# A value gather by matmul: every second panel as three fp32r passes, 1152 panel columns, five row buffers

## The chip, the cores and the metric

One core of a Trainium2 chip. The time is that of one execution on the device in microseconds (us); lower is better. Of the kernel before there are three timed runs and one profiled execution, which has a time of its own.

## What is computed

One layer of a decoder trunk on 256 + 16 tokens with 2048 features: an input projection, a gated short convolution and a chunkwise mLSTM, an output projection, and then a PEER layer. The change lies in the last part of the PEER layer. For each token, 8 heads choose 16 experts each of 16384, so that there are 128 slots per token; the reference does

```
u = peer_u[eb]
a = jax.nn.gelu(jnp.einsum('td,tkd->tk', xb, u), approximate=False)
return jnp.einsum('tk,tkd->td', wb * a, peer_v[eb])
...
h = layer_norm(ALPHA * h + ffn, ln2_g[l], ln2_b[l])
```

for two blocks ("tiles", T = 0 and 1) of 128 tokens. `peer_v` has 16384 rows (128 keys by 128) of 2048 fp32 values. All data is fp32.

## The kernel before, in words

The last stage computes the sum over slots of coefficient times row of `peer_v`, in two ways at once, by columns.

**Columns 0 to 1103 (FD = 1104), by matmul.** The coefficients are first spread out into a dense matrix of weights, `wt`, 128 x 128 x 128 for each tile: one-hot matrices of the two key indices are made on VectorE and ScalarE (`one_hots`, L1749 and L1309; `key_one_hots`, L1326), multiplied on TensorE (`place`, L935), and copied to `wt0` and `wt1` by ScalarE (`w_copy`, L1336). After that the whole of `peer_v` is streamed in 128 panels of 128 rows. SP loads panel i into `v_raw[i % 5]` (L457 to L468), when panel i - 5 is done; the first five are loaded early. TensorE's `panel(i)` (L971) does 6 fp32 matmuls, 2 tiles by 3 column cuts of 368, with `wt` as the stationary operand, and adds into 6 PSUM banks that `tile_open` (L874) filled with ALPHA * h1. The trace shows each of these fp32 matmuls as two records, 12 for a panel. `panel_done` counts panels.

**Columns 1104 to 2047 (GD = 944), by gather.** GpSimd (POOL) issues one indirect DMA for each of the 256 pairs of tile and slot (`gather_v`, L1938), which brings 128 rows of 944 values into `v_rows[n % 7]` (VRING = 7). VectorE (DVE) does `add_row(n)` (L1765): h1 += coefficient * row, one scalar_tensor_tensor, chained on its own semaphore `v_added`, since each adds to the same accumulator. Gather n waits until add n - 7 is done; gathers 3 and 4 wait for the opening of tiles 0 and 1 (their buffers lie on the part of `h1` that `tile_open` reads), gather 5 for the last one-hot product (its buffer lies on a one-hot buffer).

Each engine does its list in the order written. DVE has nothing but the 256 adds in this stage, ScalarE (ACT) nothing at all, SP the panel loads. Eight panels ahead of the last one SP also loads the two LN2 parameter rows, spread over all partitions, 1024 KB each. After the last add and the last panel DVE does the statistics and the scaling of LN2, and SP writes the output.

Earlier in the same program the projections use the form that the change brings to this stage: ScalarE copies an fp32 block to fp32r (`hi`, in `split_hi`, L992), VectorE subtracts that from the block (`lo`, in `split_lo`, L1376), and TensorE's `group` (L486) does three fp32r matmuls, high by high, high by low and low by high.

Of the kernel before, what the change touches and what calls it, by code (L numbers as in the profile page):

```python
# [16 lines left out]
F32 = mybir.dt.float32  # L17
F32R = mybir.dt.float32r
BF16 = mybir.dt.bfloat16
U32 = mybir.dt.uint32  # L20
ALU = mybir.AluOpType
ACT = mybir.ActivationFunctionType
AX = mybir.AxisListType

P = 128
D = 2048
# [3 lines left out]
NT = SEQ // P  # L30
# [3 lines left out]
PH, NKEY, TOPK = 8, 128, 16  # L34
# [41 lines left out]
BLOCKS = KT // 2  # L76
PER_UNIT = P // 4 // 8

FD = 1104
GD = D - FD  # L80
CW = 368
CUTS = tuple((a, a + CW) for a in range(0, FD, CW))
RAWS = 5
VRING = 7
WB = 4
CHUNKS_T = P // WB
OHR = 3
Y_CUTS = ((FD, D), (0, 2 * CW), (2 * CW, FD))

# [27 lines left out]
def decoder_layer(nc, x, meta_tokens, x_turned, params, w_gates, w_in, b_if, p_a, p_b, w_o, peer_wq, peer_keys, peer_u, peer_v,  # L117
# [5 lines left out]
    with ctx:  # L123
# [12 lines left out]
        def sb(name, shape, dt, at=None):  # L136
            size = int(np.prod(shape[1:])) * mybir.dt.size(dt)
            return nc.alloc_sbuf_tensor_at(name, shape, dt, offset=area(size) if at is None else at)

        KB = 1024  # L140
        a_stream = area(64 * KB)
        a_y = area(16 * KB)
        a_m = area(16 * KB)
        a_x = area(2 * KT * L * 4)
        a_yl = area(16 * KB)
        a_ml = area(16 * KB)
        a_head = area(NB * L * 4 + 10 * KB + 512)
        a_tmp = area(13 * KB)

        a_top = area(8 * KB)  # L150
# [70 lines left out]
        slots_t = sb("slots_t", [P, 3, P], F32, a_head + 12 * KB)  # L221
        neg_key = sb("neg_key", [P, P], F32R, a_head + 12 * KB + 3 * P * 4)

        wt0 = sb("wt0", [P, NKEY, P], F32, a_stream)
        assert a_head == a_ml + 16 * KB == a_yl + 32 * KB == a_x + 34 * KB + 32 * KB
        wt1 = sb("wt1", [P, NKEY, P], F32, a_x + 10 * KB)
        v_homes = [a_y + 8 * KB, a_x, a_x + FD * 4, a_tmp, a_tmp + FD * 4]
        v_raw = [sb(f"v_raw{j}", [P, FD], F32, v_homes[j]) for j in range(RAWS)]
        v_rows = [sb(f"v_rows{j}", [P, GD], F32, at) for j, at in
                  enumerate((a_top, a_top + GD * 4, a_y + 8 * KB + FD * 4, a_m, a_m + D * 4, a_y, a_y + GD * 4))]  # L230
        g2_bc = sb("g2_bc", [P, D], F32, a_stream)
        b2_bc = sb("b2_bc", [P, D], F32, a_stream + 8 * KB)
        y2 = sb("y2", [P, NT, D], F32, a_stream + 16 * KB)
# [52 lines left out]
        ps = ctx.enter_context(nc.psum_tensor("ps", [P, 8, 512], F32))  # L286
# [3 lines left out]
        def S(name):  # L290
            if name not in sems:
                sems[name] = ctx.enter_context(nc.semaphore(name))
            return sems[name]

        for n in ("set_apart ones_ready tok_in0 tok_in1 tok_in2 xt_in0 xt_in1 xt_in2 xt_in3 xt_in4 par_in bif_in gw_in keys_in bc2_in out_done "
                  "raw_in0 raw_in1 raw_in2 raw_in3 hi_ready lo_ready halves_used block_done "
                  "blocks_evacuated const_ready ln0_stats ln0_rstd mean_ready rstd_ready ln0_means ln0_rstds ln0_scaled gw_hi gw_lo x32_ready "
                  "x_split gate_w_used gates_read gate_mid gate_log gate_rows "
                  "gate_bc gate_bc_read run_ready run_out run_in pool_chain dve_chain act_chain args_ready "
                  "weights_ready masked v_transposed scores_done v_copied probs_ready num_done "  # L300
                  "recip_ready ssq_ready rms_ready hm_done hm_transposed hmt_written cc_ready sig_ready "
                  "m32_ready hi_part y_ready merged_ready tile0_done gate_used merged_used sum_ready sum_transposed merged_hi "
                  "merged_lo res_done res_ready wo_added ln1_stats ln1_rstd "
                  "ln1_nmr xn1_ready xn1_transposed h32_ready h1_turned h1_ready wq_tile wq_used wq_block "
                  "q_copied q_turned qs_ready qk_done sc_copied topk_neg topk_exp topk_done u_in0 u_in1 u_in2 u_in3 "
                  "u_in4 u_in5 u_in6 u_in7 v_in0 v_in1 v_in2 v_in3 v_in4 v_in5 v_in6 dots_done gelu_ready coef_ready "
                  "scaled tile_opened ut_turned ut_copied ut_used acc_scaled slots_turned slots_copied diff_ready "
                  "one_hot_squares one_hot_units oh_ready oh_dve_ready w_done w_evac vr_in0 vr_in1 vr_in2 vr_in3 vr_in4 "
                  "panel_done v_added ln2_stats ln2_rstd ln2_half y2_ready").split():
            S(n)  # L310
        def set_apart(eng):
# [8 lines left out]
        vr_in = [S(f"vr_in{j}") for j in range(RAWS)]  # L320
# [42 lines left out]
        def key_number(c):  # L363
            return (c - CHUNKS_T) // 2 if c >= CHUNKS_T and c % 2 else None

        def wt_rows(T, i, n):

            return (wt1 if T else wt0)[:, i:i + n, :]

        FIRST_HEADS = ((0, (0, 1)), (0, (2, 3)), (1, range(NB)))  # L370

# [110 lines left out]
        def _(pe):  # L482
# [488 lines left out]
            def panel(i):  # L971

                pe.wait_ge(vr_in[i % RAWS], 16 * (i // RAWS + 1))
                for T in range(NT):
                    for n, (a, b) in enumerate(CUTS):
                        last = mm(ps[:, 3 * T + n, 0:CW], wt_rows(T, i, 1)[:, 0, :], v_raw[i % RAWS][:, a:b], False,
                                  i == NKEY - 1)
                last.then_inc(S("panel_done"), 1)
# [7 lines left out]
        def _(act):  # L986
            chain = Steps(act, S("act_chain"))

            def A(o, i, f, **kw):
                return nc.scalar.activation(o, i, f, **kw)  # L990
# [335 lines left out]
            def key_one_hots(c):  # L1326

                act.wait_ge(S("w_done"), c - OHR + 1)
                o = oh[c % OHR]
                act.wait_ge(S("diff_ready"), key_number(c) + 1)  # L1330
                A(o[:, 1, :, :], ps[:, 5, :].rearrange("p (q i) -> p q i", q=WB), ACT.Square
                  ).then_inc(S("one_hot_squares"), 1)
                act.wait_ge(S("one_hot_squares"), CHUNKS_T + key_number(c) + 1)
                A(o[:, 1, :, :], o[:, 1, :, :], ACT.Relu, scale=-1.0, bias=one[:, 0:1]).then_inc(S("oh_ready"), 1)

            def w_copy(c):  # L1336

                act.wait_ge(S("w_done"), c + 1)
                t0 = c % CHUNKS_T * WB
                src = ps[:, 6 + (c + 1) % 2, :].rearrange("p (q i) -> p i q", q=WB)  # L1340
                A((wt0 if c < CHUNKS_T else wt1)[:, :, t0:t0 + WB], src, ACT.Copy).then_inc(S("w_evac"), 1)

            for u in range(1, 2 * PH):
                if u > FIRST_PAIR_UNIT:
# [20 lines left out]
            for c in range(CHUNKS_T, 2 * CHUNKS_T):  # L1365
                w_copy(c)
                if c % 2 == 0 and c + OHR < 2 * CHUNKS_T:
                    key_one_hots(c + OHR)


        @block.vector
        def _(dve):
            chain = Steps(dve, S("dve_chain"))
            V = nc.vector
# [374 lines left out]
            def one_hots(c):  # L1749

                dve.wait_ge(S("w_done"), c - OHR + 1)
                o = oh[c % OHR]
                t0 = c % CHUNKS_T * WB
                if key_number(c) is None:
                    V.tensor_tensor(o[:, 1, :, :], iota[:, :].unsqueeze(1).to_broadcast([P, WB, P]),  # L1755
                                    slots_t[:, 2, t0:t0 + WB].unsqueeze(2).to_broadcast([P, WB, P]), ALU.is_equal)
                for q in range(WB):
                    ins = V.tensor_scalar(o[:, 0, q, :], iota[:, :], slots_t[:, 1, t0 + q:t0 + q + 1],  # L1758
                                          slots_t[:, 0, t0 + q:t0 + q + 1], ALU.is_equal, ALU.mult)
                ins.then_inc(S("oh_dve_ready"), 1)  # L1760
# [4 lines left out]
            def add_row(n):  # L1765

                T, s = divmod(n, SLOTS)
                dve.wait_ge(v_in[n % VRING], 16 * (n // VRING + 1))
                if s:
                    dve.wait_ge(S("v_added"), n)  # L1770
                else:
                    dve.wait_ge(S("acc_scaled"), T + 1)
                V.scalar_tensor_tensor(h1[:, T, FD:D], v_rows[n % VRING][:, :], coef_all[:, T, s:s + 1], h1[:, T, FD:D],  # L1773
                                       ALU.mult, ALU.add).then_inc(S("v_added"), 1)
# [38 lines left out]
            dve.wait_ge(S("slots_copied"), 2)  # L1813
            for c in range(CHUNKS_T, 2 * CHUNKS_T):
                one_hots(c)
            for n in range(NT * SLOTS):
                add_row(n)


# [34 lines left out]
        def _(pool):  # L1854
# [83 lines left out]
            def gather_v(n):  # L1938

                if n >= VRING:  # L1940
                    pool.wait_ge(S("v_added"), n - VRING + 1)
                elif n in (3, 4):
                    pool.wait_ge(S("tile_opened"), n - 2)
                elif n == 5:
                    pool.wait_ge(S("w_done"), 2 * CHUNKS_T)
                set_apart(pool)
                Q.indirect_dma_start(v_rows[n % VRING][:, :], None, v_gathered,  # L1947
                                     bass.IndirectOffsetOnAxis(ap=idx_all[:, n:n + 1], axis=0)
                                     ).then_inc(v_in[n % VRING], 16)
# [62 lines left out]
```

## Time and profile before

| what | value |
|---|---|
| median of 3 runs | 2341.24 us (2339.43 to 2343.64) |
| the profiled execution's own time | 2348.28 us |
| its span, first to last instruction | 2346.4 us |
| PE (TensorE matmul) busy in the span | 1973.0 us, 84% |
| DVE busy | 1562.4 us, 67% |
| POOL busy | 949.0 us, 40% |
| ACT busy | 833.1 us, 36% |
| moved by DMA | 678.45 MB |

The page cuts the span into 40 slices of 58.7 us and gives the busy tenths of each; PEclk is the clock granted to TensorE, in tenths of its full speed. The stage of the change is the last nine slices or so: TensorE works there at full clock without a break, all DMA engines are busy, ScalarE is idle. "busy" of an engine counts instructions in execution; for TensorE these overlap, so its pace is read from the starts. "issue" in front of an instruction is time in which the engine waited for nothing that the profile shows. A KB in the DMA rows is 1024 bytes, a GB/s is 10^9 bytes per second.

### The profile page before, as it was taken

How to read it: one execution, taken by the hardware profiler on the slowest of the kernel's cores; microseconds unless marked ns; L12 is line 12 of the kernel's file. 1: busy time of each engine (PE TensorE's matmuls, PEld its weight loads, DVE VectorE, ACT ScalarE, POOL GpSimd, SP SyncE). 2: the span in 40 equal slices, each digit the busy share in tenths (PEclk: the TensorE clock that was granted, in tenths of full speed). 3: DMA queues.
4: the chain of work that ended last, by engine and by line, in shares of the span. 5: the costliest groups of instructions: out<-in, count | busy, mean ns of one | idle time of the engine just before them, and what ended most of it. 6: DMA issues, size and time to landing. Idle time of an engine off the chain costs nothing.

```text
span 2346.4 us, 30017 instructions
## 1 busy us (share of the span) xinstructions
PE 1973.0 (84%) x10559; PEld 1617.7 (69%) x10559; DVE 1562.4 (67%) x2234; ACT 833.1 (36%) x1369; POOL 949.0 (40%) x560
## 2 busy tenths in 40 slices
PE   8999999999999999999974242456446999999995
PEld 8888899998889988888763231345445766666663
DVE  7444455555445554554899999999988766666667
ACT  6444443444444444445122121586767300000000
POOL 0000000000000000000558888888874488788874
PEclk9999999999999999999997566676667999999998
DMA  7544465565565565556999999999996499999996
GB/s 245 162 143 142 141 197 184 177 181 186 191 196 180 180 197 182 195 179 233 380 390 377 421 412 412 406 421 416 418 421 261 190 412 411 411 409 411 411 410 274
DMA packets 213884, 678.45 MB, mean 289 GB/s; under 512 B 14712, under 2 KB 64256, under 8 KB 180224
## 3 DMA queue, kind: packets, MB, share of 16 engines
q0 software_dynamic: 57664, 394.31, 41.4%
q1 hardware_dynamic: 156112, 282.75, 35.8%
q8 instruction: 62, 1.02, 0.2%
q14 instruction: 46, 0.38, 0.0%
HBM read 674.89 MB, written 2.11 MB: 289 GB/s over the span
## 4 chain that ended last, share of the span: by engine, by line
PE 46%; issue 23%; POOL 11%; DMA 11%; DVE 8%; ACT 1%; DVEq 0%; POOLq 0%; ACTq 0%
PE ps L484 45%; DMA u_rows<-in_peer_u,idx_all 8%; POOL v_rows L1947 7%; POOL u_rows L1934 4%; DMA v_rows<-in_v_gathered,idx_all 2%; DVE junk L1725 2%; DVE ohs L1758 1%; DVE h L1773 1%; ACT hi L990 0%; DVE ohs L1755 0%; DVE ki L1678 0%; DVE scw L1679 0%; DVE ki L1685 0%; ACT h1t L990 0%; PE ps L625 0%
## 5 line engine op out<-in xcount | busy, mean ns | idle before, releaser
L1380 DVE TENSOR_TENSOR lo<-raw,hi 128x1024 fp32r<-128x1024 f32 x344 | 419.5, 1225 | 478.6 <-ACT hi L990 478.0
L1934 POOL DMA_INDIRECT u_rows<-in_peer_u,idx_all x256 | 532.6, 2081 | 153.2 <-issue 67.1
L990 ACT ACTIVATE hi<-raw 128x1024 fp32r<-128x1024 f32 x348 | 368.2, 1060 | 533.4 <-PE ps L484 532.1
L1725 DVE SCALAR_TENSOR_TENSOR junk<-u_rows,h 128x2048 bf16<-128x2048 f32 x228 | 520.0, 2282 | 45.1 <-DMA u_rows<-in_peer_u,idx_all 44.8
L484 PE MATMUL ps<-v_raw,wt 128*128 128x368 f32 x1536 | 477.1, 474 | 2.0 <-DMA v_raw<-in_peer_v 1.9
L1947 POOL DMA_INDIRECT v_rows<-in_v_gathered,idx_all x256 | 394.1, 1539 | 145.3 <-issue 79.5
L484 PE MATMUL ps<-xh,hi 128*128 128x256 f32 (+2 forms) x1536 | 438.9, 286 | 1.2 <-issue 0.9
L484 PE MATMUL ps<-xh,lo 128*128 128x256 f32 (+2 forms) x1536 | 435.2, 283 | 0.0
L484 PE MATMUL ps<-xl,hi 128*128 128x256 f32 (+2 forms) x1536 | 434.4, 283 | 0.0
L1773 DVE SCALAR_TENSOR_TENSOR h<-v_rows,coef_all,h 128x944 f32<-128x944 f32 x256 | 307.6, 1202 | 176.8 <-DMA v_rows<-in_v_gathered,idx_all 174.9
L484 PEld LDWEIGHTS ps<-v_raw,wt 128*128 128x128 f32 x1536 | 292.4, 190 | 186.7 <-DMA v_raw<-in_peer_v 2.5
L1874 POOL TENSOR_TENSOR rstd<-rstd,m_half 128x1 f32<-128x1 f32 (+1 forms) x7 | 5.4, 764 | 818.6 <-DVE rstd L1643 798.5
L484 PEld LDWEIGHTS ps<-xh,hi 128*128 128x128 f32 x1536 | 289.9, 189 | 6.5 <-issue 5.6
L484 PEld LDWEIGHTS ps<-xl,hi 128*128 128x128 f32 x1536 | 290.2, 189 | 0.0
L484 PEld LDWEIGHTS ps<-xh,lo 128*128 128x128 f32 x1536 | 289.6, 189 | 0.0
L903 PE MATMUL ps<-ident,u_rows 128*128 128x128 f32 x448 | 81.2, 321 | 182.9 <-issue 158.8
L484 PE MATMUL ps<-ohs 128*128 128x128 f32 x512 | 101.2, 361 | 128.2 <-ACT ohs L990 126.2
L903 PEld LDWEIGHTS ps<-ident,u_rows 128*128 128x128 f32 x448 | 68.3, 170 | 197.4 <-issue 188.7
L484 PEld LDWEIGHTS ps<-ohs 128*128 128x128 f32 x512 | 88.9, 259 | 142.6 <-ACT ohs L990 136.5
L990 ACT ACTIVATE ut<-ps 128x512 f32<-128x512 f32 x112 | 66.9, 597 | 263.8 <-PE ps L903 261.7
L484 PE MATMUL ps<-ut,h1t 128*128 128x256 f32 x448 | 131.4, 426 | 0.1
L484 PE MATMUL ps<-hi,xh 128*128 128x512 f32 x256 | 101.7, 397 | 1.8 <-DVE t_y L1558 1.3
(224 smaller groups left out, 2364.3 us busy)
## 6 DMA issues: line engine op xcount, KB each, us to landing
raw<-in_w_in SPq DMA_DIRECT2D x96, 1024.0 KB, 5.3
v_raw<-in_peer_v SPq DMA_DIRECT2D x128, 552.0 KB, 7.7
raw<-in_w_in SPq DMA_DIRECT2D x64, 256.0 KB, 3.3
raw<-in_w_in SPq DMA_DIRECT2D x32, 512.0 KB, 4.7
raw<-in_p_a SPq DMA_DIRECT2D x16, 1024.0 KB, 5.0
raw<-in_p_b SPq DMA_DIRECT2D x16, 1024.0 KB, 5.1
raw<-in_w_o SPq DMA_DIRECT2D x16, 1024.0 KB, 5.1
wq_raw<-in_peer_wq SPq DMA_DIRECT2D x16, 1024.0 KB, 9.7
```

Source lines behind the costliest of these rows:

```text
L484: return nc.tensor.matmul(o, a, b, start=start, stop=stop)
L903: last = nc.tensor.transpose(ps[:, 3 + g % 2, (2 * n + r) * P:(2 * n + r + 1) * P], u_rows[row_slot(u, k)][:, kt * P:(kt + 1) * P], ident[ ...
L990: return nc.scalar.activation(o, i, f, **kw)
L1380: V.tensor_tensor(raw_lo[:, hh // 2, k4, :] if kept else lo[:, hh % SLOT_N, :, :], raw[:, hh // 2, k4, :], (kept_hi(hh) if kept else hi[:, ...
L1725: V.scalar_tensor_tensor(junk[:, n % 2, :], u_rows[row_slot(u, k)][:, :], 1.0, h1[:, u // PH, :], ALU.mult, ALU.mult, accum_out=dots[:, u ...
L1758: ins = V.tensor_scalar(o[:, 0, q, :], iota[:, :], slots_t[:, 1, t0 + q:t0 + q + 1], slots_t[:, 0, t0 + q:t0 + q + 1], ALU.is_equal, ALU.mult)
L1773: V.scalar_tensor_tensor(h1[:, T, FD:D], v_rows[n % VRING][:, :], coef_all[:, T, s:s + 1], h1[:, T, FD:D], ALU.mult, ALU.add).then_inc(S(" ...
L1874: Q.tensor_tensor(rstd[:cnt, n:n + 1], rstd[:cnt, n:n + 1], m_half[:cnt, 0:1], ALU.pow).then_inc(S(name + "_rstd"), 1)
L1934: Q.indirect_dma_start(u_rows[slot][:, :], None, peer_u, bass.IndirectOffsetOnAxis(ap=idx_all[:, n:n + 1], axis=0)).then_inc(u_in[slot], 16)
L1947: Q.indirect_dma_start(v_rows[n % VRING][:, :], None, v_gathered, bass.IndirectOffsetOnAxis(ap=idx_all[:, n:n + 1], axis=0)).then_inc(v_in ...
```

## The change

- FD goes from 1104 to 1152 columns: matmul cuts of 384, panels of 576 KB, gathered rows of 896 columns. VRING goes from 7 to 5; the two row buffers that lay on `h1` are dropped, for the high parts of v (`v_hi`, two buffers) lie there now. `wt0` and `wt1` become two ends of one tensor, so that one instruction can read panel i's weights of both tiles.
- For each odd panel i (64 of them, numbered n = i // 2), ACT copies `v_raw` (1152 columns) to `v_hi` in fp32r and the weights of both tiles (2 x 128) to `w_hi`; it waits for the panel's load and for panel i - 4, which used the same `v_hi`. DVE subtracts the high parts, v in place over `v_raw` (`v_lo`), the weights into `w_lo`. TensorE does 18 fp32r matmuls of 384 columns (2 tiles, 3 passes, 3 cuts) in place of 6 fp32 matmuls. Even panels stay fp32.
- DVE's two subtractions for panel i stand amid the adds: panel 1 ahead of add 2, panel 3 ahead of add 4, then panel 5 ahead of add 6, panel 7 ahead of add 10, and so on each fourth add, up to panel 127 ahead of add 250. So panel i is split ahead of add 2i - 4.
- Gather 3 now waits for the last one-hot product, so three gathers go out early; then gather n waits for add n - 5.

The diff (semaphore names, `wt_rows` and `w_copy`'s renamed target left out):

```diff
-FD = 1104
+FD = 1152
-CW = 368
+CW = 384
-VRING = 7
+VRING = 5
...
+        v_lo = [sb(f"v_lo{j}", [P, FD], F32R, v_homes[j]) for j in range(RAWS)]
         v_rows = [sb(f"v_rows{j}", [P, GD], F32, at) for j, at in
-                  enumerate((a_top, a_top + GD * 4, a_y + 8 * KB + FD * 4, a_m, a_m + D * 4, a_y, a_y + GD * 4))]
+                  enumerate((a_top, a_top + GD * 4, a_y + 8 * KB + FD * 4, a_y, a_y + GD * 4))]
+        v_hi = [sb(f"v_hi{j}", [P, FD], F32R, a_m + j * D * 4) for j in range(2)]
+        w_hi = [sb(f"w_hi{j}", [P, NT, P], F32R, a_head + (8 + j) * KB) for j in range(2)]
+        w_lo = [sb(f"w_lo{j}", [P, NT, P], F32R, a_head + (10 + j) * KB) for j in range(2)]
...
+        def split_number(i):
+            return i // 2 if i % 2 else None
...
                 pe.wait_ge(vr_in[i % RAWS], 16 * (i // RAWS + 1))
+                if split_number(i) is not None:
+                    b = split_number(i) % 2
+                    pe.wait_ge(S("v_lo_ready"), split_number(i) + 1)
+                    for T in range(NT):
+                        for w, v in ((w_hi[b], v_hi[b]), (w_hi[b], v_lo[i % RAWS]), (w_lo[b], v_hi[b])):
+                            for n, (c0, c1) in enumerate(CUTS):
+                                last = mm(ps[:, 3 * T + n, 0:CW], w[:, T, :], v[:, c0:c1], False,
+                                          i == NKEY - 1 and w is w_lo[b])
+                    last.then_inc(S("panel_done"), 1)
+                    return
...
+            def split_panel(i):
+
+                n = split_number(i)
+                if n < 2:
+                    act.wait_ge(S("tile_opened"), n + 1)
+                else:
+                    act.wait_ge(S("panel_done"), i - 4 + 1)
+                act.wait_ge(vr_in[i % RAWS], 16 * (i // RAWS + 1))
+                A(v_hi[n % 2][:, :], v_raw[i % RAWS][:, :], ACT.Copy)
+                if n == 0:
+                    act.wait_ge(S("w_done"), 2 * CHUNKS_T)
+                    act.wait_ge(S("w_evac"), 2 * CHUNKS_T)
+                A(w_hi[n % 2][:, :, :], wt_tiles(i), ACT.Copy).then_inc(S("v_hi_ready"), 1)
...
+            def split_panel(i):
+
+                n = split_number(i)
+                dve.wait_ge(S("v_hi_ready"), n + 1)
+                V.tensor_tensor(v_lo[i % RAWS][:, :], v_raw[i % RAWS][:, :], v_hi[n % 2][:, :].bitcast(F32), ALU.subtract)
+                V.tensor_tensor(w_lo[n % 2][:, :, :], wt_tiles(i), w_hi[n % 2][:, :, :].bitcast(F32), ALU.subtract
+                                ).then_inc(S("v_lo_ready"), 1)
+
             for n in range(NT * SLOTS):
+                if n == 2:
+                    split_panel(1)
+                elif n == 4:
+                    split_panel(3)
+                elif 4 < n < 2 * NKEY - 4 and n % 4 == 2:
+                    split_panel((n + 2) // 2 + 1)
                 add_row(n)
...
                 if n >= VRING:
                     pool.wait_ge(S("v_added"), n - VRING + 1)
-                elif n in (3, 4):
-                    pool.wait_ge(S("tile_opened"), n - 2)
-                elif n == 5:
+                elif n == 3:
                     pool.wait_ge(S("w_done"), 2 * CHUNKS_T)
```

## Rows read from the trace of the kernel before

**Rows 1.** The page: slices of the span (58.7 us each).
```profile
PE   8999999999999999999974242456446999999995
DVE  7444455555445554554899999999988766666667
PEclk9999999999999999999997566676667999999998
GB/s 245 162 143 142 141 197 184 177 181 186 191 196 180 180 197 182 195 179 233 380 390 377 421 412 412 406 421 416 418 421 261 190 412 411 411 409 411 411 410 274
```

**Rows 2.** Windows: us; busy PE, PEld, DVE, ACT, POOL (records); clock, DMA share, GB/s.
```profile
400.00:500.00 100.00, 100.00 (x836) 99.66 (x835) 52.98 (x61) 41.04 (x43) 0.00 (x0) 1.00 0.60 183
600.00:700.00 100.00, 100.00 (x437) 81.84 (x436) 46.70 (x41) 45.54 (x45) 0.00 (x0) 1.00 0.58 189
1291.00:1350.00 59.00, 15.31 (x72) 12.87 (x72) 55.85 (x103) 8.50 (x14) 47.68 (x25) 0.59 1.01 421
1900.00:2280.00 380.00, 380.00 (x1231) 233.53 (x1230) 241.96 (x202) 0.00 (x0) 311.36 (x203) 1.00 1.02 410
```

**Rows 3.** Waits, 1900 to 2280 us: who for whom, us, times, longest.
```profile
DVE h L1773 <- DMA v_rows<-in_v_gathered,idx_all: 137.9, 201, 1.8
```

**Rows 4.** DMA issues of the page: KB each, median us to landing.
```profile
v_raw<-in_peer_v SPq DMA_DIRECT2D x128, 552.0 KB, 7.7
```

**Rows 5.** Groups from 1842 us on: busy us, mean ns of one, idle before.
```profile
L484 PE MATMUL ps<-v_raw,wt 128*128 128x368 f32 x1536 | 477.1, 474 | 2.0 <-DMA v_raw<-in_peer_v 1.9
L1845 DVE SCALAR_TENSOR_TENSOR y<-h,mv,g_bc 128x944 f32<-128x944 f32 x2 | 2.4, 1200 | 0.0
L1845 DVE SCALAR_TENSOR_TENSOR y<-ps,mv,g_bc 128x736 f32<-128x736 f32 x2 | 2.0, 980 | 0.0
```

**Rows 6.** Groups, 400 to 500 us.
```profile
L484 PE MATMUL ps<-xh,hi 128*128 128x258 f32 x191 | 54.2, 284 | 0.0
L1380 DVE TENSOR_TENSOR lo<-raw,hi 128x1024 fp32r<-128x1024 f32 x35 | 42.5, 1225 | 44.1 <-ACT hi L990 44.0
L990 ACT ACTIVATE hi<-raw 128x1024 fp32r<-128x1024 f32 x35 | 37.1, 1060 | 54.0 <-PE ps L484 53.9
```

**Rows 7.** Timeline of TensorE, the first and the last of 13 matmuls in a row.
```profile
600.42 0.40 PE L484 MATMUL ps<-hi,xh 128*128 128x512 f32 x1
...
603.20 0.40 PE L484 MATMUL ps<-hi,xh 128*128 128x512 f32 x1
```

**Rows 8.** Group of VectorE, 1300 to 1600 us.
```profile
L1708 DVE TENSOR_TENSOR ohv<-oh_k,kif 128x256 f32<-128x256 f32 x15 | 5.7, 415 | 0.0
```

**Rows 9.** Timeline of the steady stage: start us, us, engine, what, idle before.
```profile
2053.47 1.20 DVE L1773 SCALAR_TENSOR_TENSOR h<-v_rows,coef_all,h 128x944 f32<-128x944 f32 x1 [0.50 <-DMA v_rows<-in_v_gathered,idx_all]
2054.09 1.40 POOL L1947 DMA_INDIRECT v_rows<-in_v_gathered,idx_all  x1 [0.30 <-issue]
2055.45 1.20 DVE L1773 SCALAR_TENSOR_TENSOR h<-v_rows,coef_all,h 128x944 f32<-128x944 f32 x1 [0.78 <-DMA v_rows<-in_v_gathered,idx_all]
2055.79 1.68 POOL L1947 DMA_INDIRECT v_rows<-in_v_gathered,idx_all  x1 [0.30 <-issue]
```

**Rows 10.** Timeline of the stage's start.
```profile
1842.52 5.17 DVE L1773 SCALAR_TENSOR_TENSOR h<-v_rows,coef_all,h 128x944 f32<-128x944 f32 x4
...
1844.57 40.77 PE L484 MATMUL ps<-v_raw,wt 128*128 128x368 f32 x131
1845.31 1.89 POOL L1947 DMA_INDIRECT v_rows<-in_v_gathered,idx_all  x1 [43.19 <-PE ps L484]
...
1850.43 1.20 DVE L1773 SCALAR_TENSOR_TENSOR h<-v_rows,coef_all,h 128x944 f32<-128x944 f32 x1 [2.74 <-DMA v_rows<-in_v_gathered,idx_all]
```

**Rows 11.** Timeline of the stage's end.
```profile
2295.67 27.93 PE L484 MATMUL ps<-v_raw,wt 128*128 128x368 f32 x84 [1.93 <-DMA v_raw<-in_peer_v]
...
2316.62 10.34 DVE L1773 SCALAR_TENSOR_TENSOR h<-v_rows,coef_all,h 128x944 f32<-128x944 f32 x8 [0.87 <-DMA v_rows<-in_v_gathered,idx_all]
...
2327.00 1.45 DVE L1832 BATCH_NORM_STATS2 st<-ps 128x6 f32<-128x368 f32 x3
```

More of the change, by code:

```diff
@@ L222, in decoder_layer @@
         neg_key = sb("neg_key", [P, P], F32R, a_head + 12 * KB + 3 * P * 4)
-        wt0 = sb("wt0", [P, NKEY, P], F32, a_stream)
         assert a_head == a_ml + 16 * KB == a_yl + 32 * KB == a_x + 34 * KB + 32 * KB
-        wt1 = sb("wt1", [P, NKEY, P], F32, a_x + 10 * KB)
         v_homes = [a_y + 8 * KB, a_x, a_x + FD * 4, a_tmp, a_tmp + FD * 4]
         v_raw = [sb(f"v_raw{j}", [P, FD], F32, v_homes[j]) for j in range(RAWS)]
+        v_lo = [sb(f"v_lo{j}", [P, FD], F32R, v_homes[j]) for j in range(RAWS)]
         v_rows = [sb(f"v_rows{j}", [P, GD], F32, at) for j, at in
-                  enumerate((a_top, a_top + GD * 4, a_y + 8 * KB + FD * 4, a_m, a_m + D * 4, a_y, a_y + GD * 4))]
+                  enumerate((a_top, a_top + GD * 4, a_y + 8 * KB + FD * 4, a_y, a_y + GD * 4))]
+        v_hi = [sb(f"v_hi{j}", [P, FD], F32R, a_m + j * D * 4) for j in range(2)]
+        w_hi = [sb(f"w_hi{j}", [P, NT, P], F32R, a_head + (8 + j) * KB) for j in range(2)]
+        w_lo = [sb(f"w_lo{j}", [P, NT, P], F32R, a_head + (10 + j) * KB) for j in range(2)]
+        wt_gap = (a_x + 10 * KB - a_stream) // (P * 4)
+        wt_both = sb("wt_both", [P, wt_gap + NKEY, P], F32, a_stream)
         g2_bc = sb("g2_bc", [P, D], F32, a_stream)
@@ L305, in decoder_layer @@
                   "q_copied q_turned qs_ready qk_done sc_copied topk_neg topk_exp topk_done u_in0 u_in1 u_in2 u_in3 "
-                  "u_in4 u_in5 u_in6 u_in7 v_in0 v_in1 v_in2 v_in3 v_in4 v_in5 v_in6 dots_done gelu_ready coef_ready "
+                  "u_in4 u_in5 u_in6 u_in7 v_in0 v_in1 v_in2 v_in3 v_in4 dots_done gelu_ready coef_ready "
                   "scaled tile_opened ut_turned ut_copied ut_used acc_scaled slots_turned slots_copied diff_ready "
-                  "one_hot_squares one_hot_units oh_ready oh_dve_ready w_done w_evac vr_in0 vr_in1 vr_in2 vr_in3 vr_in4 "
+                  "one_hot_squares one_hot_units oh_ready oh_dve_ready w_done w_evac vr_in0 vr_in1 vr_in2 vr_in3 vr_in4 v_hi_ready v_lo_ready "
                   "panel_done v_added ln2_stats ln2_rstd ln2_half y2_ready").split():
@@ L364, in key_number, with wt_tiles @@
             return (c - CHUNKS_T) // 2 if c >= CHUNKS_T and c % 2 else None
+        def split_number(i):
+            return i // 2 if i % 2 else None
+        def wt_tiles(i):
+            return wt_both[:, i:i + wt_gap + 1:wt_gap, :]
         def wt_rows(T, i, n):
-            return (wt1 if T else wt0)[:, i:i + n, :]
+            return wt_both[:, T * wt_gap + i:T * wt_gap + i + n, :]
         FIRST_HEADS = ((0, (0, 1)), (0, (2, 3)), (1, range(NB)))
@@ L1340, in w_copy @@
                 src = ps[:, 6 + (c + 1) % 2, :].rearrange("p (q i) -> p i q", q=WB)
-                A((wt0 if c < CHUNKS_T else wt1)[:, :, t0:t0 + WB], src, ACT.Copy).then_inc(S("w_evac"), 1)
+                A(wt_rows(c // CHUNKS_T, 0, NKEY)[:, :, t0:t0 + WB], src, ACT.Copy).then_inc(S("w_evac"), 1)
             for u in range(1, 2 * PH):
@@ L1368, in _ @@
                     key_one_hots(c + OHR)
+            def split_panel(i):
[10 more added lines that the diff above has]
+                A(w_hi[n % 2][:, :, :], wt_tiles(i), ACT.Copy).then_inc(S("v_hi_ready"), 1)
+            for i in range(NKEY):
+                if split_number(i) is not None:
+                    split_panel(i)
         @block.vector
```

## The prediction

> **What bounds the kernel now.** I read the page's slices first [rows 1]: before the last nine slices nothing changes, so only the stage from about 1842 us on counts. There TensorE is full, VectorE two thirds busy, and the DMA engines move about 410 GB/s. The windows come next [rows 2]: in the 380 us from 1900 to 2280, 1231 matmul records and 202 adds, DMA share 1.02. So a panel takes 12 x 380 / 1231 = 3.70 us on TensorE, and two adds (a panel's worth: 256 adds to 128 panels) take 2 x 380 / 202 = 3.76 us. The third view is the waits [rows 3]: 201 of the 202 adds wait for their gather, 137.9 us in all. TensorE hardly waits for its panels (1.9 us in the stage, [rows 5]), which land 7.7 us after issue [rows 4] with 5 buffers of 3.7 us each. So two bounds lie on one another: TensorE at 7.41 us for two panels, and DMA, through the gathers, at 7.52 us. The last add ends at 2326.96, the last matmul at about 2323.6 [rows 11], and LN2 starts at 2327.00. The adds, and so DMA, set the end, TensorE 3.4 us behind. A change has to relieve both.
>
> **The change, part by part,** in units of two panels and four adds (64 units).
>
> *TensorE.* An fp32 matmul of 368 columns starts every 2 x 308.7 ns; at 384 columns a record takes 308.7 x 384 / 368 = 322 ns, a full panel 12 x 0.322 = 3.86 us. For the split panel: fp32r matmuls of 256 to 258 columns start every 100 / 836 = 119.6 ns, those of 512 columns, by the starts of the 1st and the 13th of a run, every (603.20 - 600.42) / 12 = 232 ns [rows 2, 6, 7]. Between them, 384 columns take 175 ns, and 18 of them 3.15 us. A unit is 7.01 us against 7.41. TensorE gains 0.40 x 64 = 26 us, if nothing holds it. Alone it is worth nothing, since DMA ends last.
>
> *DMA.* A unit moves 2 x 552 + 4 x 472 = 2992 KB now (944 columns x 4 bytes x 128 rows are 472 KB), and 2 x 576 + 4 x 448 = 2944 KB after: a factor of 0.984. From add 4 at 1850.43 to add 248 at 2316.62 [rows 10, 11] it is 466.2 us; 1.6% of it is **7.5 us less**. At 7.40 us for a unit DMA stays the bound; TensorE has 0.39 us to spare.
>
> *Early loads.* Now 4 rows and 5 panels are in before the stage (4 adds run at once, the fifth waits, [rows 10]): 4648 KB. After: 3 rows and 5 panels, 4224 KB. The 424 KB move into the stage: 434 kB / 410 GB/s = **1.1 us more**.
>
> *VectorE.* Adds: 944 against 736 columns cost 1200 and 980 ns [rows 5], 1.06 ns a column, so 896 columns take 1.15 us. Eight adds back to back took 10.34 us, so 1.305 from start to start [rows 11]: 1.25 after. Subtraction: 1024 columns at 1225 ns [rows 6], 1152 at 1.36 us; 256 columns at 0.42 [rows 8], of which some 0.35 shows behind another. A split is 1.7 us. A unit: 4 x 1.25 + 1.7 = 6.7 us of 7.40. VectorE goes from 70% (5.22 of 7.52) to 91%, still under the bound; the cover is its 0.7 us of waiting in each unit. The last eight adds are 0.05 shorter each: **0.4 less**. Without the DMA bound it would be TensorE at 7.01 that is next, then VectorE at 6.7.
>
> *ScalarE* has nothing to do in the stage. 1152 columns at 1060 ns per 1024 [rows 6] are about 1.2 us, 256 more about 0.4: 1.6 us of 7.4. It matters as latency. The raw panel i is ordered when panel i - 5 ends, lands up to 7.7 us later, is copied (1.6) and subtracted (1.7): 11.0 us, plus semaphores. TensorE wants it 4 panels, 14.8 us, after the order. About 3.5 us to spare, and VectorE may come to the split anywhere in that interval; where it comes early it waits, and the adds behind it, and the gathers behind these.
>
> *POOL and the ring.* Here a price is unknown. In the steady stage a gather ends 0.82 us after the end of the add that ran when it started (2054.67 to 2055.49, 2056.65 to 2057.47, [rows 9]), and the next starts 0.30 later. So the slot of an add that ends at t is refilled by a gather that ends near t + 2.7 (1.12 to its start, a mean of 311.36 / 203 = 1.53 in it, [rows 2]). The longest hold grows from an add of 1.20 to a subtraction of 1.36. The round trip of a row is 7 x 1.88 = 13.2 us now, of which 1.2 add, 2.7 POOL, 9.3 landing and queue. After it has to be 5 x 1.85 = 9.25 us: 1.15 add, 2.7 POOL, **5.4 us for the landing**. The nearest quick one is at the start: gather 4 ends at 1847.20, its add starts at 1850.43, 3.2 us [rows 10]. What lies between 3.2 and 9.3 is queue: now about 5 rows and 2 panels are in flight, 3.5 MB, which is 8.5 us at 410 GB/s. With two rows fewer and a panel sooner on its way, some 1.9 MB (2.4 rows, 1.4 panels) are left, 4.6 us, and DMA stays fed. I take 1 us for all losses of coupling and for the start, where the splits of panels 1 and 3 fall between adds while the ring fills. Ends: 0 (the rings smooth it all) and 20 us (the second rival).
>
> The shared port of VectorE and GpSimd gives those holds a name: by the Trainium skill (SBUF — State Buffer, "SBUF: two separate sides") a VectorE operation with two SBUF inputs locks out a GpSimd operation that reads SBUF until it ends. The rows agree with it on the adds; by it each of the 128 subtractions is one more hold, and the sum would lose what the ring cannot take up, as in the second rival.
>
> *Before the stage:* 4% more columns in the 12 matmuls that open the tiles, of 5.8 us for ten at the lower clock, gives **0.2 more**. Output, LN2: the same columns in other cuts, nothing.
>
> **Sum:** -7.5 + 1.1 - 0.4 + 1.0 + 0.2 = -5.6 us. Against the profiled execution's own 2348.28 us (span 2346.4 and 1.9 around it) that is 2342.7; it was 7.0 us above the median of the runs, so against 2341.24 it is **2335.6 us**, 0.24% faster. I count 0.2% (4.7 us) as what a measurement can tell from no change.
>
> **Rivals.**
>
> *A higher rate of DMA.* Rows of 2048 columns in the u stage moved at 421 GB/s, at a DMA share of 1.01 [rows 2]; the 1104 and 944 columns move at 410. If 1152 and 896 columns run like those, a unit is 7.40 x 410 / 421 = 7.21 us, still above TensorE's 7.01: 64 x 0.19 = 12 us more, 2323.5. For it: 1152 and 896 columns are whole multiples of 256 bytes, 1104 and 944 are not. Against: the u rows are also longer, 8 KB apiece, and their stage runs on other work. 0.15. The Trainium skill has such a rule (DMA: Bandwidth & Descriptors, "How a descriptor splits into AXI transactions": a descriptor that starts off a 256-byte boundary fetches unused bytes); the trace shows only the two rates and not their cause.
>
> *The ring of five starves (slower).* Place: a gather's landing in the steady stage. It decides from 5.4 us on. At 5.8 us a row needs (1.15 + 2.7 + 5.8) / 5 = 1.93 us instead of 1.85, and 252 rows 20 us more: 2355.6. For it: 9.3 us of landing today, and a pause of 1.7 us at each split, behind which rows queue up and then want new gathers at once. TensorE, held by splits that stand among late adds, follows. Against: the queue shrinks with what is in flight. 0.28.
>
> *The gain is lost without a loss.* VectorE at 91% must take each gather when it lands; its waits on a late high part plus the ring eat 3 to 8 us, and the time stays within 2337 to 2344. 0.12.
>
> *That the change does not do what it says* (fp32r passes as dear as fp32 ones) would show as 18 x 0.64 us for a panel; the projections' pace excludes it. Nor should TensorE's clock fall: the slices show it low only where TensorE was 20 to 60% busy, and 0.9 where it was 70% busy [rows 1]; here it will be 95% busy, with short gaps.
>
> **How the numbers follow.** Forecast case 0.45: 2331 to 2340, two thirds of it faster by over 0.2%, one third within (0.30 and 0.15). Higher rate 0.15, all faster. Starved ring 0.28, slower. Lost gain 0.12: 0.05 faster, 0.07 within. Sum: faster 0.50, within 0.2% 0.22, slower 0.28. The range goes from the second case's 2323.5 to most of the third: 2323 to 2354. The likeliest case's own is 2331 to 2340.
>
> **What would show it.** In the profile after: DMA share still 1.02 at 410 GB/s, 4 adds in 7.4 us, adds that wait on gathers for about 0.7 us a unit in all, matmul starts at 0.322 and 0.175 us, short waits of TensorE of 0.4 us a unit, full clock. Wrong: a DMA share of 0.97 or less with VectorE waiting on gathers (starved ring), VectorE waiting on ScalarE ahead of its subtractions (late high parts), a rate near 421 (second case), TensorE without waits (my prices for it too low).

## The result, and the profile after

The changed kernel takes 2362.24 us (median of 6 runs, 2359.16 to 2366.42) against 2342.93 us for the kernel before (6 runs): ratio 1.0087, 95% interval 1.0076 to 1.0098. It is 19.3 us **slower**. The forecast was 5.6 us faster, and the range ended at 2354. The case that came about is the rival with the ring of five, at a price near the one given for it (20 us).

The slices of the page after, to be laid beside [rows 1]:

```profile
PE   8999999999999999999964424455557999999985
DVE  7444455554444545554899999999989787778777
PEclk9999999999999999999987666667577999999998
GB/s 243 165 138 142 145 198 176 194 162 201 189 195 180 190 183 196 182 187 248 394 369 409 422 416 419 415 414 416 399 421 155 296 391 394 378 391 395 379 384 263
```

Up to slice 30 nothing of weight has changed. In the last nine slices the granted clock is still full, VectorE is busier, as meant, and the rate of DMA has dropped from 410 to somewhere between 378 and 395 GB/s. The windows from 1850 to 1900 and 1900 to 2280 us give it exactly (columns as in [rows 2]):

```profile
1850.00:1900.00 50.00, 48.17 (x207) 36.74 (x206) 36.21 (x36) 10.32 (x14) 28.32 (x25) 1.00 1.00 387
1900.00:2280.00 380.00, 354.07 (x1470) 262.74 (x1469) 299.16 (x294) 72.15 (x98) 247.22 (x196) 1.00 1.00 387
```

Against [rows 2] this is the whole result in one line. VectorE's 294 operations are 98 of the splits and 196 adds, where there were 202 in the same time: four adds take 4 x 380 / 196 = 7.76 us instead of 7.52. Note the DMA share: 1.00 after, 1.02 before. It counts the time that packets take, and looks full in both; only the GB/s tell that 6% of the rate is gone. TensorE is busy 354 us of 380 and waits for the rest.

Who waits for whom, 1900 to 2280 us (us in total, times, longest), beside [rows 3]:

```profile
ACT v_hi L1010 <- DMA v_raw<-in_peer_v: 291.4, 46, 10.5
POOL v_rows L1997 <- DVE h L1811: 92.3, 67, 2.6
DVE h L1811 <- DMA v_rows<-in_v_gathered,idx_all: 76.8, 105, 2.1
...
POOL v_rows L1997 <- issue: 40.8, 129, 1.8
PE ps L494 <- DVE w_lo L1859: 25.7, 33, 2.5
...
```

ScalarE's wait costs nothing; it has nothing else to do. The second and the third row belong together. Before, POOL waited 3.4 us for VectorE in this window, that is, a free buffer was nearly always there. Now it waits 92.3 us for an add to free one, and VectorE waits 76.8 us for a row to land. That fits a ring of row buffers that is too short, each end waiting for the other and the DMA engines between them with too little to do. By themselves these two rows do not show it, though: the version with seven buffers below, which keeps DMA full, has 76.9 and 62.9 us in them. What sets the changed kernel apart is the rate of 387 GB/s. TensorE comes third, it waits for splits that stand among the late adds.

The landings after (from issue, median us), and the chain that ended last, 1900 to 2340 us, with four of its longest pieces:

```profile
v_raw<-in_peer_v SPq DMA_DIRECT2D x128, 576.0 KB, 7.5
v_rows<-in_v_gathered,idx_all POOLq DMA_INDIRECT x256, 7.4
```

```profile
by line: DMA v_rows<-in_v_gathered,idx_all 49.2%; issue 22.8%; DVE h L1811 15.1%; POOL v_rows L1997 6.6%; DMA v_raw<-in_peer_v 3.1%; DVE w_lo L1859 2.4%; PE ps L494 2.0%; DVE v_lo L1858 0.3%; ACT v_hi L1010 0.3%; POOLq L318 0.1%; ACT w_hi L
...
2048.22 8.70 DMA v_rows<-in_v_gathered,idx_all
2056.94 1.16 DVE h L1811
2058.29 1.90 POOL v_rows L1997
2063.14 8.02 DMA v_rows<-in_v_gathered,idx_all
```

Landing, add, POOL, landing: the chain runs through the round trip of a row buffer. (Between the third and the fourth line POOL issues the gathers that piled up behind its wait, at 2058.29, 2060.49, 2061.89 and 2063.14.) A row takes 380 / 196 = 1.94 us, so five buffers go round in 9.69 us: about 7.4 from issue to landing, 1.15 in the add, 1.1 from the add's end to the next issue (median). The forecast needed 9.25.

One turn of it in the timeline of the steady stage after:

```profile
2056.94 1.15 DVE L1811 SCALAR_TENSOR_TENSOR h<-v_rows,coef_all,h 128x896 f32<-128x896 f32 x1 [2.12 <-DMA v_rows<-in_v_gathered,idx_all]
2058.01 1.35 DVE L1858 TENSOR_TENSOR v_lo<-v_raw,v_hi 128x1152 fp32r<-128x1152 f32 x1
2058.29 1.90 POOL L1997 DMA_INDIRECT v_rows<-in_v_gathered,idx_all  x1 [2.64 <-DVE h L1811]
2059.19 1.16 ACT L1010 ACTIVATE v_hi<-v_raw 128x1152 fp32r<-128x1152 f32 x1 [7.64 <-DMA v_raw<-in_peer_v]
2059.28 0.42 DVE L1859 TENSOR_TENSOR w_lo<-wt_both,w_hi 128x256 fp32r<-128x256 f32 x1
2059.62 2.40 DVE L1811 SCALAR_TENSOR_TENSOR h<-v_rows,coef_all,h 128x896 f32<-128x896 f32 x2
2059.84 1.30 PE L494 MATMUL ps<-v_hi,w_hi 128*128 128x384 f32 x3 [2.48 <-DVE w_lo L1859]
```

VectorE waits 2.12 us for a row, adds it, and turns to the split, while the next two rows land and have to wait for it (the two adds at 2059.62 run back to back). POOL waited 2.64 us for a free buffer; the gather that it then issues at 2058.29 is held by the subtraction that runs from 2058.01 to 2059.36, and ends 0.82 us behind it, at 2060.19. TensorE waits 2.48 us for the same split. Short windows around that wait:

```profile
2059.00:2063.00 4.00, 3.16 (x10) 3.19 (x11) 3.19 (x5) 1.47 (x2) 3.22 (x3) 0.59 0.89 310
2064.00:2068.00 4.00, 4.00 (x16) 2.67 (x15) 2.93 (x4) 1.47 (x2) 2.62 (x3) 1.00 0.93 353
```

DMA moves 310 and 353 GB/s here, and the granted clock behind the wait is 0.59, mostly at the lower of its two levels (1.2 GHz), before it is full again. In the 380 us the clock rounds to 1.00, so this is rare.

### The profile page after: what moved, and what is told of

It reads as the page before. It is cut to its first block, busy times and chain, and to the rows that moved or that the text cites. A ratio compares the mean times of both kernels' runs of the same rounds, so it can differ in the third digit from the quotient of the medians.

```text
span 2363.2 us, 31170 instructions
## 1 busy us (share of the span) xinstructions
PE 1954.7 (83%) x10943; PEld 1666.7 (71%) x10943; DVE 1647.3 (70%) x2362; ACT 926.7 (39%) x1497; POOL 886.6 (38%) x560
## 4 chain that ended last, share of the span: by engine, by line
PE 46%; DMA 19%; issue 17%; DVE 11%; POOL 5%; ACT 1%; SPq 0%; DVEq 0%; POOLq 0%; ACTq 0%
PE ps L494 45%; DMA v_rows<-in_v_gathered,idx_all 10%; DMA u_rows<-in_peer_u,idx_all 8%; POOL u_rows L1986 4%; DVE h L1811 3%; DVE junk L1763 2%; POOL v_rows L1997 1%; DVE ohs L1796 1%; DMA v_raw<-in_peer_v 1%; DVE w_lo L1859 0%; ACT hi L1010 0%; DMA raw<-in_w_in 0%; DVE ohs L1793 0%; DVE ki L1716 0%; DVE scw L1717 0%
## 5 line engine op out<-in xcount | busy, mean ns | idle before, releaser
L1986 POOL DMA_INDIRECT u_rows<-in_peer_u,idx_all x256 | 540.2, 2110 | 145.4 <-issue 68.7
L1763 DVE SCALAR_TENSOR_TENSOR junk<-u_rows,h 128x2048 bf16<-128x2048 f32 x228 | 519.6, 2280 | 44.2 <-DMA u_rows<-in_peer_u,idx_all 42.8
L1997 POOL DMA_INDIRECT v_rows<-in_v_gathered,idx_all x256 | 324.2, 1266 | 236.0 <-DVE h L1811 129.8
L1811 DVE SCALAR_TENSOR_TENSOR h<-v_rows,coef_all,h 128x896 f32<-128x896 f32 x256 | 294.6, 1151 | 109.6 <-DMA v_rows<-in_v_gathered,idx_all 102.9
L494 PE MATMUL ps<-v_raw,wt_both 128*128 128x384 f32 x768 | 258.3, 486 | 0.0
L1010 ACT ACTIVATE v_hi<-v_raw 128x1152 fp32r<-128x1152 f32 x64 | 74.6, 1166 | 396.8 <-DMA v_raw<-in_peer_v 367.1
L494 PEld LDWEIGHTS ps<-v_raw,wt_both 128*128 128x128 f32 x768 | 144.8, 190 | 85.5 <-ACT wt_both L1010 0.7
```

What stands on the lines that cost most here:

```text
L494: return nc.tensor.matmul(o, a, b, start=start, stop=stop)
L1763: V.scalar_tensor_tensor(junk[:, n % 2, :], u_rows[row_slot(u, k)][:, :], 1.0, h1[:, u // PH, :], ALU.mult, ALU.mult, accum_out=dots[:, u ...
L1986: Q.indirect_dma_start(u_rows[slot][:, :], None, peer_u, bass.IndirectOffsetOnAxis(ap=idx_all[:, n:n + 1], axis=0)).then_inc(u_in[slot], 16)
```

## The experiments

Two theories at first. **R**: five row buffers starve the gathers by themselves. **S**: VectorE's pause at each split does it. All ratios are to the kernel before, run beside on the same chip.

### Five buffers in the kernel before

```diff
-VRING = 7
+VRING = 5
...
-                  enumerate((a_top, a_top + GD * 4, a_y + 8 * KB + FD * 4, a_m, a_m + D * 4, a_y, a_y + GD * 4))]
+                  enumerate((a_top, a_top + GD * 4, a_y + 8 * KB + FD * 4, a_y, a_y + GD * 4))]
...
-                elif n in (3, 4):
-                    pool.wait_ge(S("tile_opened"), n - 2)
-                elif n == 5:
+                elif n == 3:
```

> The kernel before with five row buffers instead of seven (gather 3 waits for the last one-hot product, gather n for add n - 5), nothing else. Theory R (the ring of five alone starves the gathers): a row's round trip cannot shrink below about 9.5 us, so a row takes 1.9 us or a little more and the time is 2352 to 2362 us, the DMA rate of the steady stage falls below 400 GB/s. Rival S (VectorE's pause at each split does it, the ring alone is harmless): 2343 to 2347 us, rate 408 to 411.

Measured: 2358.69 us, ratio 1.0070 (1.0053 to 1.0086), 16 us slower. No split, no new column, and most of the loss is there. (One row fewer is loaded early too, 483 kB, an estimated 1.2 us at 410 GB/s.) The window and the landings of this run, and TensorE's last piece and the last add:

```profile
1900.00:2280.00 380.00, 380.00 (x1230) 233.52 (x1229) 232.93 (x195) 0.00 (x0) 272.10 (x195) 1.00 1.01 401
...
v_rows<-in_v_gathered,idx_all POOLq DMA_INDIRECT x256, 7.4
...
2299.79 17.79 PE L484 MATMUL ps<-v_raw,wt 128*128 128x368 f32 x57
2337.22 1.20 DVE L1773 SCALAR_TENSOR_TENSOR h<-v_rows,coef_all,h 128x944 f32<-128x944 f32 x1 [0.24 <-DMA v_rows<-in_v_gathered,idx_all]
```

195 adds, 5 x 380 / 195 = 9.74 us for the trip, the same 7.4 us of landing. TensorE keeps its pace here, since no panel waits for a place among the adds. So the panels run ahead: the last matmul ends at 2317.6, the last add at 2338.4, and from 2320 to 2340 us the rows alone move 236 GB/s. That is why the window still shows 401 GB/s, where a rate below 400 was expected: with 97.5 panels, as many as go with 195 adds, in place of 102.5 it would be an estimated 393. R holds; S alone is out.

### Seven buffers in the changed kernel

```diff
-VRING = 5
+VRING = 7
...
-        v_homes = [a_y + 8 * KB, a_x, a_x + FD * 4, a_tmp, a_tmp + FD * 4]
+        v_homes = [a_y + 8 * KB, a_x, a_x + FD * 4, a_top, a_y]
+        a_late = a_head + 12 * KB
...
+                  enumerate((a_y + 8 * KB + FD * 4, a_top + FD * 4, a_late + GD * 4, a_late + 2 * GD * 4,
+                             a_late + 3 * GD * 4, a_late, a_y + FD * 4))]
...
-                elif i == 3:
-                    sp.wait_ge(S("dots_done"), 2 * PH * TOPK)
+                elif i == 4:
+                    sp.wait_ge(S("w_done"), 2 * CHUNKS_T)
...
-                elif n == 3:
+                elif n == 2:
+                    pool.wait_ge(S("dots_done"), 2 * PH * TOPK)
+                elif n == 5:
                     pool.wait_ge(S("w_done"), 2 * CHUNKS_T)
```

> The changed kernel with seven row buffers: same columns, same splits, the buffers laid out anew (two panels and five rows ahead of the last one-hot product; panel 4 now waits for that product too). Theory R: the round trip may last 13 us again, DMA is full, 2328 to 2340 us. Rival S: VectorE's pauses stay, 2352 to 2362 us.

Measured: 2340.04 us, ratio 0.9991 (0.9982 to 1.0001). 22.2 us come back. (By its trace four panels, where the text above says two, and five rows are ordered ahead of the last one-hot product, 4544 KB; that is 320 KB more than in the changed kernel, an estimated 0.8 us.) Its window, waits and landing:

```profile
1900.00:2280.00 380.00, 368.18 (x1535) 273.02 (x1533) 311.20 (x305) 75.12 (x102) 255.77 (x204) 1.00 1.02 407
...
POOL v_rows L2002 <- DVE h L1814: 76.9, 51, 4.0
DVE h L1814 <- DMA v_rows<-in_v_gathered,idx_all: 62.9, 99, 1.8
...
v_raw<-in_peer_v SPq DMA_DIRECT2D x128, 576.0 KB, 8.2
v_rows<-in_v_gathered,idx_all POOLq DMA_INDIRECT x256, 10.4
```

DMA is at 407 GB/s and a share of 1.02, four adds take 7.45 us, and a landing may last 10.4 us without harm. The time lies at the upper end of what was expected.

### No subtraction, with five and with seven buffers

```diff
-                    pe.wait_ge(S("v_lo_ready"), split_number(i) + 1)
+                    pe.wait_ge(S("v_hi_ready"), split_number(i) + 1)
...
-                if n == 2:
-                    split_panel(1)
...
```

> The changed kernel with VectorE's two subtractions left out; TensorE does its 18 fp32r matmuls on the high parts alone, so the low parts are missing from the result. Five row buffers. Theory R: little is won, 2352 to 2362 us. Rival S: without the pauses 2328 to 2340 us.

> The seven-buffer version (1152 columns) with VectorE's two subtractions left out; TensorE does its 18 matmuls on the high parts, so the low parts are missing from the result. With five buffers leaving them out gave 5 us back. Theory R: with seven buffers DMA is the bound and the pauses are hidden, 2336 to 2341 us (the seven-buffer version: 2340.0). Rival S2 (the pauses cost on their own): 2333 us or less.

Measured with five: 2356.78 us, 1.0057 (1.0040 to 1.0074), 5.5 us less than the changed kernel. With seven: 2338.73 us, 0.9979 (0.9970 to 0.9989), 1.3 us less than the seven-buffer version, which these runs hardly tell. With seven buffers the pauses are all but hidden, though VectorE is 82% busy by the window of that version (311.20 of 380). The window with five buffers and no subtraction:

```profile
1900.00:2280.00 380.00, 375.67 (x1605) 291.07 (x1604) 217.81 (x190) 78.59 (x107) 265.61 (x188) 0.99 1.01 399
```

The 5.5 us are not simply the price of the pauses. Without the subtractions there are 190 adds in the window, fewer than the 196 with them; what goes faster is TensorE, with 1605 records where there were 1470, for the edit also unties a panel from its place among the adds. TensorE then ends at 2294.4, the last add at 2337.2, and in that tail the rows alone move 304 GB/s at most (2310 to 2320 us). So the rate of 399 GB/s against 387 is panels taken sooner, not rows. The ring of five costs 16 us in the kernel before, 18 without the subtractions (2356.78 less 2338.73) and 22 with them: most of the loss is the ring's own. How much of the rest is the pauses and how much the tie, no run here tells.

### Six buffers, in both kernels

In the changed kernel a sixth home on the one-hot scratch, with three rows and five panels early as before; in the kernel before one home fewer.

```diff
-VRING = 5
+VRING = 6
...
-        v_homes = [a_y + 8 * KB, a_x, a_x + FD * 4, a_tmp, a_tmp + FD * 4]
+        a_late = a_head + 12 * KB
+        v_homes = [a_y + 8 * KB, a_x, a_x + FD * 4, a_late + GD * 4, a_late + (GD + FD) * 4]
...
-                  enumerate((a_top, a_top + GD * 4, a_y + 8 * KB + FD * 4, a_y, a_y + GD * 4))]
+                  enumerate((a_top, a_top + GD * 4, a_y + 8 * KB + FD * 4, a_y, a_y + GD * 4, a_late))]
```

> The changed kernel with six row buffers (the sixth on a part of the one-hot scratch, panels 3 and 4 moved up behind it), three rows early as before. Theory R (threshold): a row's round trip of about 9.7 us at five buffers leaves room once 6 x 1.86 = 11.2 us are allowed, so most of the loss comes back: 2339 to 2346 us, landing from issue 8.5 to 9 us. Rival P (each buffer brings its share, half of the 22 us): 2350 to 2354 us.

> The kernel before with six row buffers instead of seven. Five gave 16 us more. Theory R (threshold between five and six): 2341 to 2346 us. Rival P (a share for each buffer): 2349 to 2352 us.

Measured: 2341.07 us, 0.9993 (0.9984 to 1.0003), and 2341.01 us, 0.9989 (0.9980 to 0.9998). All of the loss comes back with one buffer, and the seventh adds nothing that these runs can tell. Landing from issue in the changed kernel: 7.4 us with five, 8.6 with six, 10.4 with seven. With six:

```profile
1900.00:2280.00 380.00, 368.09 (x1528) 271.40 (x1528) 311.44 (x306) 73.67 (x100) 257.18 (x204) 1.00 1.02 405
...
v_rows<-in_v_gathered,idx_all POOLq DMA_INDIRECT x256, 8.6
```

Rival P, a share for each buffer, is out: it is a threshold, between five and six. Since the early loads are those of the changed kernel here, the step from six buffers to five costs 2362.2 - 2341.1 = 21 us in it.

### The other two parts, each alone, with seven buffers

Splits alone (FD = 1104, CW = 368), then columns alone (FD = 1152, `split_number` always None, no `split_panel` on VectorE):

> The splits alone: the seven-buffer layout at the old 1104 panel columns, every second panel in three fp32r passes. TensorE is relieved (6.7 us of 7.5 in a unit), DMA moves the same 2992 KB a unit. Theory D (DMA was the bound before, TensorE only lay beside it): 2341 to 2347 us, no gain. Rival T (TensorE was the true bound): 2330 us or less.

> The columns alone: seven buffers, 1152 panel columns, every panel in fp32, no split. TensorE needs 7.7 us a unit, 64 units: 494 us, where the whole stage took 482. Theory: TensorE binds, 2353 to 2360 us, DMA share about 0.99. Rival (TensorE's pace was set by DMA even so): 2341 us or less.

Measured: 2343.27 us, 1.0005 (0.9996 to 1.0015), and 2357.75 us, 1.0069 (1.0052 to 1.0086). Their windows, in this order:

```profile
1900.00:2280.00 380.00, 353.46 (x1523) 264.84 (x1522) 317.44 (x303) 73.10 (x102) 257.52 (x203) 1.00 1.02 411
...
1900.00:2280.00 380.00, 380.00 (x1180) 223.89 (x1179) 242.96 (x212) 0.00 (x0) 310.75 (x211) 1.00 1.02 407
...
2336.32 1.49 DVE L1881 BATCH_NORM_STATS2 st<-ps 128x6 f32<-128x384 f32 x3 [34.95 <-PE ps L497]
```

In the first, TensorE is idle 26 us of 380 and nothing is faster: DMA was a bound of its own. In the second, 1180 records in 380 us are 0.322 us each, 3.86 for a panel; TensorE binds and is 15 us late. In the same window 212 adds were done, so the gathers ran ahead, and at the end VectorE waits 34.95 us for TensorE's last panel. The DMA share was 1.02 even so, not the 0.99 expected: while the gathers run ahead, DMA is full as well. Both halves of the change are needed together, as the forecast had it.

### More columns

> As the seven-buffer version, with 1176 panel columns: a unit of two panels and four rows is 2920 KB instead of 2944, TensorE 7.16 us instead of 7.01, rows of 3488 and 4704 bytes, no multiples of 256. If bytes alone count: 3 to 4 us faster than the seven-buffer version with 1152 columns. If rows on 256-byte boundaries are faster (rate above 411 GB/s with 1152): slower than that version by 5 us or more.

> Seven buffers, splits, 1200 panel columns: 2896 KB a unit, TensorE 18 x 0.182 + 12 x 0.336 = 7.31 us against DMA's 7.3. If bytes alone count, as the step from 1152 to 1176 suggests (2.4 us per 24 columns): 2335 us. If TensorE now binds: 2338 to 2342 us.

Measured: 1176 columns 2337.62 us, 0.9976 (0.9967 to 0.9986); 1200 columns 2338.33 us, 0.9985 (0.9976 to 0.9995). From 1152 to 1176 it is 2.4 us where 3 to 4 were expected; from 1176 to 1200 nothing that these runs can tell. The rate is 407 GB/s with 1152, 1176 and 1200 alike, so 256-byte boundaries bring nothing that can be seen. With 1104 columns it was 411 in the same layout, and the columns alone, without splits, had 407: the rate falls with the step from 1104 to 1152 columns, and no run here shows why. At 1200 TensorE has no idle time left:

```profile
1900.00:2280.00 380.00, 380.00 (x1562) 288.87 (x1561) 314.07 (x312) 77.16 (x102) 252.49 (x209) 1.00 1.02 407
```

### A version that beats both

```diff
-                if i == NKEY - 8:
+                if i == NKEY - 1:
```

on top of seven buffers, splits and 1176 columns; and the same edit alone in the kernel before.

> Meant to beat both kernels: seven buffers, splits, 1176 panel columns, and the two LN2 parameter rows (2 MB) loaded behind the last panel instead of behind panel 120. There DMA has time to spare. If DMA is the bound until the last panel is loaded: 2 MB at 407 GB/s are 5.2 us, and 2332 to 2334 us against 2337.6. If the end hangs on the last adds alone: 2336 to 2338 us.

> The kernel before with the LN2 parameter rows loaded behind the last panel, nothing else, to tell that edit's share. If the 5 us of DMA count here as well: 2336 to 2339 us. If TensorE's own 479 us of panels hold the end: 2340 to 2343 us.

Measured: 2335.43 us, 0.9960 (0.9947 to 0.9974), 7.9 us under the 2343.31 of the kernel before beside it and 27 under the changed one; and 2341.95 us, 0.9991 (0.9982 to 1.0000). The late load brings some 2 us of the 5 that were possible, hardly more than these runs can tell; in the kernel before its gain is within that. The estimate of 2332 to 2334 was too good. By the trace, DMA does not yet have time to spare behind the last panel's order: the parameter rows are asked for at 2291.2 us, the last gather starts at 2303.3, and a gather of 2295.99 lands 12.12 us later. That the parameter rows delay these last gathers is a reading of the trace, which no run here tests.

## Why the prediction was wrong, point by point

- **Two bounds on one another, TensorE and DMA.** Right. Splits alone gave nothing, columns alone cost 15 us.
- **TensorE's price.** Right. A unit of a full and a split panel was put at 7.01 us; the timeline after has 6.99 (a full panel starts at 1848.33 and the next at 1855.32, with no wait between):

```profile
1848.33 4.03 PE L494 MATMUL ps<-v_raw,wt_both 128*128 128x384 f32 x12
...
1855.32 4.03 PE L494 MATMUL ps<-v_raw,wt_both 128*128 128x384 f32 x12
```

- **VectorE's price.** Right: adds of 1.151 us, subtractions of 1.352 and 0.418, where 1.15, 1.36 and 0.42 stood.
- **DMA's gain of 7.5 us, less 1.1 for the early loads.** Right in sign, too large. With the ring out of the way and the early loads equal in number, the step from 1104 to 1152 columns is 2343.3 to 2340.0, 3.2 us, where 7.5 stood. The forecast kept the rate; it fell from 411 to 407 GB/s, 1% of 466 us or some 4.6 us, and four adds take 7.45 us, not 7.40. That two more steps of 24 columns gave -2.4 and +0.7 us shows where TensorE takes over.
- **The step that failed: "I take 1 us for all losses of coupling", in the part on POOL and the ring.** It measured 21 us (five buffers against six), a little beyond the upper end of 20. The condition was put rightly: a row's landing must come down to 5.4 us behind POOL's end, or the ring starves. What was wrong is the value. I took the 9.3 us of before for a queue that would shrink to 4.6 us with what is in flight, for rows and panels alike. It shrank to 7.4 from issue, some 6.1 behind POOL's mean of 1.27: 0.7 us more than allowed, and the panels' landing hardly shrank, 7.7 us before, 7.5 after. So 7.5 / 3.88 = 1.9 panels and 6.1 / 1.94 = 3.1 rows are on their way, where the forecast had left 1.4 and 2.4. In the forecast's own terms, 5.4 needed, 6.1 found; POOL's part was 2.4 (1.1 and 1.27) and not 2.7, so the trip is 9.69 and not 9.25, and 252 rows at 0.09 us more make about 22 us. The rival priced 5.8 at 20 us, about the price that came.
- **The weighing.** The ends of that cost lay 20 us apart, and the value was put beside the lower one, on an argument about queues that no row supported. The one row for a quick landing (3.2 us, [rows 10]) came from a moment when at first no panel was on its way: five were in, and the sixth is ordered at 1848.6. The row of the same stage said 9.3, and halfway would already have been over the threshold. That the rival came out near its price is in part luck: it put 5.8 us of landing and 2.7 of POOL where 6.1 and 2.4 were found. The range, too, should have reached to what that rival priced, 2355.6, and beyond; it stopped at 2354.
- **The sign named for a starved ring,** a DMA share of 0.97 or less, did not come: the share was 1.00. What told was the rate.
- **The higher rate of DMA.** Out: 407 GB/s at 1152, 1176 and 1200 columns, less than the 411 at 1104. By the Trainium skill (DMA: Bandwidth & Descriptors, "How a descriptor splits into AXI transactions") a descriptor that does not start on a 256-byte boundary fetches bytes that go unused; on rows of 3.4 to 4.8 KB no run here shows a gain from whole multiples.
- **The shared port.** The subtraction holds a gather just as an add does: the gather ends 0.82 us behind its end (2058.29, above). By the Trainium skill (SBUF — State Buffer, "SBUF: two separate sides") a VectorE operation with two SBUF inputs fully blocks a GpSimd operation that reads SBUF, and the trace agrees. The gathers were no dearer for it: POOL's mean is 1.27 us after, 1.40 with five buffers and no split, 1.54 before.

Not settled is what the 6 to 8 us of landing under load consist of. In the split kernels rows took 7.4, 8.6 and 10.4 us with five, six and seven buffers, panels 7.5, 7.7 and 8.2; a fixed part and a shared queue both fit.

## What to carry to other kernels

A ring of buffers for transfers under a full DMA has a threshold: the round trip (landing from issue, use, time to the next issue) divided by the pace wanted, rounded up. Here the trip of the starved ring gives 9.7 / 1.86 = 5.2, so six. The trip read from the kernel before, 13.2 us, would have said eight: with a buffer to spare, part of the landing is the ring's own queue. So a trip read from the loaded stage errs to the safe side, and one built on a quiet moment to the other; the landing did shrink, from 9.3 us to 6.1, but not to 5.4. One buffer below the threshold cost 21 us, one above it gave nothing. When buffers are given up to make room for a new operand, price that first: the memory was there, in scratch that was dead by then.

## What the runs showed of the hardware that was not expected

- Over a long window the DMA share hardly shows starvation. It was 1.00 at 387 GB/s, 1.01 at 401 and 1.02 at 410. Nor do POOL's waits for a free buffer tell by themselves: they are 3.4 us before and 52.1 with five buffers there, but 92.3, 73.5 and 76.9 us in the split kernels with five, six and seven, and of these only the first starves. The GB/s told the difference.
- In the split kernels the panels' landing grows little with the number of row buffers (7.5, 7.7, 8.2 us with five, six, seven), while the rows' grows much (7.4, 8.6, 10.4). The number of buffers is not all of it: without splits, seven gave 7.7 and 9.2, and without the subtractions five gave 8.1 and 7.6.
- One wait of TensorE of 2.48 us was followed by a granted clock of 0.59 over 4 us; the other gaps of the 380 us, 26 us in all with it and none of them above 1.75 us, left the mean at 1.00.
